# A chunked mLSTM stage rewritten to take its heads two at a time

## The reference

```
    log_d = jnp.where(lower, b[..., :, None] - b[..., None, :] + li[..., None, :], -jnp.inf)
    m_t = jnp.maximum(a, jnp.max(log_d, axis=-1))
    s = jnp.einsum('bhctk,bhcsk->bhcts', qc, kc) * jnp.exp(log_d - m_t[..., None])
    e_int = jnp.exp(a - m_t)
    num = (jnp.einsum('bhcts,bhcsv->bhctv', s, vc)
           + e_int[..., None] * jnp.einsum('bhcvk,bhctk->bhctv', C_prev, qc))
    den = jnp.sum(s, axis=-1) + e_int * jnp.einsum('bhck,bhctk->bhct', n_prev, qc)
    h = num / jnp.maximum(jnp.abs(den), jnp.exp(-m_t))[..., None]
...
        C_new = a[..., None, None] * C + e[..., None, None] * Cl
        n_new = a[..., None] * n + e[..., None] * nl
```

## Time and profile before

| what | value |
|---|---|
| median of three runs | 3321.8 us |
| time of the profiled execution | 3317.97 us |
| its span | 3316.2 us |
| TensorE busy in the span | 86% |
| VectorE busy | 52% |
| ScalarE busy | 35% |
| GpSimd busy | 25% |
| mean granted TensorE clock | 0.904 of full |

### The profile page before, as it was taken

The page is one execution under the profiler, slowest core; times in us unless marked ns, Lnnn a source line. Parts: engine busy times, 40 slices in busy tenths (PEclk is TensorE's granted clock), DMA queues, the critical chain, the costliest instruction groups (busy, mean ns, idle before and its releaser), DMA issues. The chain is left out here.

```text
span 3316.2 us, 39108 instructions
## 1 busy us (share of the span) xinstructions
PE 2861.8 (86%) x12086; PEld 2025.9 (61%) x12087; DVE 1726.0 (52%) x2710; ACT 1168.1 (35%) x1598; POOL 840.4 (25%) x1036
## 2 busy tenths in 40 slices
PE   4999969968787999999999993998987999883897
PEld 4455446647536777777777772446664666673776
DVE  3667845556535556756666554036644111435653
ACT  1100011123205556656666553005513111213653
POOL 0100021122173333333343332038320000103333
PEclk9999955569798999999999996999998999986999
DMA  5321100003316878978888865300011111316873
GB/s 217 103 102 54 54 0 1 1 29 142 152 65 226 276 225 271 316 252 300 306 274 295 249 165 168 113 0 1 27 15 51 38 44 33 135 70 223 306 232 59
DMA packets 159184, 463.49 MB, mean 140 GB/s; under 512 B 37964, under 2 KB 67264, under 8 KB 138328
## 3 DMA queue, kind: packets, MB, share of 16 engines
q1 hardware_dynamic: 115816, 358.12, 29.2%
q0 software_dynamic: 43264, 104.02, 13.1%
HBM read 414.31 MB, written 91.62 MB: 153 GB/s over the span
## 5 line engine op out<-in xcount | busy, mean ns | idle before, releaser
L1829 DVE TENSOR_TENSOR moe_low<-moe_raw,moe_high 128x2048 fp32r<-128x2048 f32 x160 | 359.5, 2288 | 80.6 <-ACT moe_high L1774 80.6
L1739 PE MATMUL psum<-moe_high,moe_xg_high 128*128 128x512 f32 x960 | 389.9, 406 | 6.1 <-issue 3.1
L1741 PE MATMUL psum<-moe_high,moe_xg_low 128*128 128x512 f32 x960 | 378.3, 394 | 0.0
L1740 PE MATMUL psum<-moe_low,moe_xg_high 128*128 128x512 f32 x960 | 375.5, 391 | 0.0
L1774 ACT ACTIVATE moe_high<-moe_raw 128x2048 fp32r<-128x2048 f32 x160 | 297.5, 1914 | 0.1
L1675 POOL DMA_INDIRECT moe_acc<-moe_y_blk,moe_is_now x97 | 216.2, 2229 | 303.6 <-DMA moe_acc<-moe_y_blk,moe_is_now 273.0
L1786 ACT ACTIVATE moe_y_blk<-psum,row_w 128x1024 f32 x124 | 138.1, 1113 | 232.7 <-DMA moe_acc<-moe_y_blk,moe_is_now 129.1
L1726 PE MATMUL psum<-moe_high_down,moe_hid_high 128*128 x488 | 208.3, 427 | 12.7 <-DVE moe_hid_low L1838 12.6
L1713 PE MATMUL psum<-ident,moe_xg 128*128 128x128 f32 x976 | 132.5, 280 | 96.8 <-DMA moe_xg<-moe_rows,moe_ig_now 96.8
L1739 PEld LDWEIGHTS psum<-moe_high,moe_xg_high 128*128 128x128 f32 x960 | 181.7, 189 | 43.1 <-issue 4.8
L1741 PEld LDWEIGHTS psum<-moe_high,moe_xg_low 128*128 128x128 f32 x960 | 180.8, 188 | 43.1
(11 more groups left out here) (574 smaller groups left out, 5305.3 us busy)
## 6 DMA issues: line engine op xcount, KB each, us to landing
moe_raw<-in_we_gate SPq DMA_DIRECT2D x64, 1024.0 KB, 7.7
moe_raw<-in_we_up SPq DMA_DIRECT2D x64, 1024.0 KB, 11.4
moe_raw<-in_we_down SPq DMA_DIRECT2D x64, 1024.0 KB, 7.5
moe_raw<-in_w_e_gate SPq DMA_DIRECT2D x16, 1024.0 KB, 7.0
moe_raw<-in_w_e_up SPq DMA_DIRECT2D x16, 1024.0 KB, 10.1
moe_raw<-in_w_e_down SPq DMA_DIRECT2D x16, 1024.0 KB, 8.7
w_ring<-in_w_in SPq DMA_DIRECT2D x12, 1024.0 KB, 7.3
wada<-in_w_ada SPq DMA_DIRECT2D x8, 1024.0 KB, 10.5
```

Source lines behind the costliest of these rows:

```text
L1739: pe.matmul(to, x_hi, R(of_k(w_hi, k)), start=(k == 0), stop=False)
L1740: pe.matmul(to, x_hi, R(of_k(w_lo, k)), start=False, stop=False)
L1741: last = pe.matmul(to, x_lo, R(of_k(w_hi, k)), start=False, stop=(k == KD - 1))
L1829: dve.tensor_tensor(R(low[:, at:at + 2048]), raw[r][:, part], hi, ALU.subtract).then_inc(w_low, 1)
```

## The change

The list of units becomes a list of pairs: chunk step j, direction d, pair of heads k, 40 in all; p is the index of a pair and v = p - 8 counts the 32 with outputs. The two heads of a pair, i = 0 and 1, have their keys and queries on partitions 0 to 63 and 64 to 127.

- The two local products go to the two column halves of bank 7, and one DVE instruction over 128 partitions updates the state of both heads. `EA2` holds their factors side by side. Bank 7 is the only one for local products, so that the local products of p wait for the state of p - 1.
- The two score products, and the two state products, go to the two row halves of the array and to two banks each.
- The running maxima of all four heads of a step and a direction are spread by one product of 512 columns (L801) every second pair, with `NM4`, in which each head's rows stand apart, and `of_group`. DVE adds the mask to the four at once (L887); E is now the bias of ACT's four exponentials (L853).
- DVE's product with the scores, the sum, and the three steps for the divisor are one instruction for two heads. ACT's scaling (L865), POOL's scaling and the final division (L920, L922) stay one instruction per head.

```
-    units = [(j, d, h) for j in range(STEPS) for d in range(2) for h in range(H1)]
+    pairs = [(j, d, k) for j in range(STEPS) for d in range(2) for k in range(H1 // 2)]
...
+                def maxima(g):
+
+                    pe.matmul(s.bank[6][:, :], of_group[:, NC * 2 + g:NC * 2 + g + 1].to_broadcast([NCOL, P]), NM4[:, :, :],
+                              start=True, stop=True).then_inc(maxima_done, 1)
+
                 def scores(v):
...
+                    for i in range(2):
+                        last = pe.matmul(s.bank[i][:, 0:P], s.qkT[lanes(i), 2 + k, t0:t0 + P], s.qkT[lanes(i), k, t0:t0 + P],
+                                         start=True, stop=True)
+                    last.then_inc(scores_done, 1)
...
+                    if p < PS:
+                        pe.wait_ge(wv_ready, 2 * (p + 1))
+                        if p >= 1:
+                            pe.wait_ge(state_moved, p)
+                        for i in range(2):
+                            h = 2 * k + i
+                            last = pe.matmul(s.bank[7][lanes(i), 0:W], s.k_tok[:, tile_of(j, d), h * DK:(h + 1) * DK],
+                                             wv[:, p % 2, i, :], start=True, stop=True)
+                        last.then_inc(local_done, 1)
                     if v >= 0:
...
                         if v >= 2:
                             pe.wait_ge(combined, v - 1)
+                        pe.wait_ge(state_moved, p - H1 + 1)
+                        for i in range(2):
+                            pe.matmul(s.bank[bank + i][:, 256:256 + W], s.qkT[lanes(i), k, t0:t0 + P], state[lanes(i), d, k, :],
+                                      start=True, stop=True)
                         pe.wait_ge(pt_ready, v + 1)
+                        if v + 1 < NV:
+                            scores(v + 1)
+                        for i in range(2):
+                            last = pe.matmul(s.bank[bank + i][:, 0:W], pt[:, v % 2, i, :], s.v_aug[:, tile_of(j, d), 2 * k + i, :],
+                                             start=True, stop=True)
+                        last.then_inc(num_done, 1)
+                        if v % 2 == 0 and v + 2 < NV:
+                            pe.wait_ge(masked, v // 2 + 1)
+                            maxima(v // 2 + 1)
...
+                for p, (j, d, k) in enumerate(pairs):
+                    v = p - P0
+                    if v % 2 == 1 and 0 <= v + 1 < NV:
+                        mask((v + 1) // 2)
                     if 0 <= v + 1 < NV:
                         weights(v + 1)
                     if v >= 0:
+                        dve.wait_ge(inter_ready, 2 * (v + 1))
+                        H, D2 = hsum[:, v % 2, :, :], dn[:, v % 2, :, :]
+                        dve.tensor_tensor(H, both(out_banks(v))[:, :, 0:W], inter[:, v % 2, :, :], ALU.add).then_inc(combined, 1)
...
+                    if p < PS:
+                        dve.wait_ge(local_done, p + 1)
+                        C = state[:, d, k, :]
+                        dve.scalar_tensor_tensor(C, C, EA2[:, j, d, k:k + 1], s.bank[7][:, 0:W],
                                                  ALU.mult, ALU.add).then_inc(state_moved, 1)
```

More of the change, by code:

```diff
@@ L844, in _, with exps @@
[L844 to L851, removed]
-                        act.activation(inter[:, v % 2, :], s.bank[2 + v % 2][:, 256:256 + W], ACT.Copy,
+                def exps(g):
+                    j, d, _ = pairs[P0 + 2 * g]
+                    act.wait_ge(masked, g + 1)
+                    for h in range(H1):
+                        one = decay[:, g % 2, h, :]
+                        act.activation(one, one, ACT.Exp, bias=s.E[:, j, d, h:h + 1]).then_inc(exp_ready, 1)
@@ new lines, in _ @@
+                exps(0)
+                for v in range(NV):
+                    j, d, k = pairs[P0 + v]
+                    if v % 2 == 1 and v + 1 < NV:
+                        exps(v // 2 + 1)
+                    act.wait_ge(num_done, v + 1)
+                    if v >= 2:
+                        act.wait_ge(combined, v - 1)
+                    for i in range(2):
+                        h = 2 * k + i
+                        act.activation(inter[:, v % 2, i, :], s.bank[out_banks(v) + i][:, 256:256 + W], ACT.Copy,
@@ L857, in _ @@
                 c = s.dve_c
-                c.link(dve, dve.memset(state[:, :, :, :], 0.0))
-                dve.wait_ge(masks_set, 2)
-                def decay(v):
-                    j, d, h = out_unit(v)
+                heads = lambda i: s.EA[lanes(i), :, :, :].rearrange("p j d (k i) -> p (j d k) i", i=2)[:, :, i]
+                unit = s.ident[0:NCOL, 0:NCOL]
+                c.then(dve.memset(state[:, :, :, :], 0.0))
+                for i in range(2):
+                    c.then(dve.tensor_copy(EA2[lanes(i), :, :, :].rearrange("p j d k -> p (j d k)"), heads(i)))
@@ new lines, in _ @@
+                c.then(dve.tensor_reduce(of_group[:, :], unit.rearrange("p (g h) -> p g h", h=H1), AX_X, ALU.add))
+                c.link(dve, dve.tensor_reduce(of_head[:, :], unit.rearrange("p (g h) -> p h g", h=H1), AX_X, ALU.add))
+                for h in range(H1):
+                    c.then(dve.tensor_scalar(NM4[:, h, :], s.NMT[:, :], of_head[:, h:h + 1], None, ALU.mult))
+                c.wait(dve)
+                dve.sem_inc(maxima_set, 1)
+                dve.wait_ge(masks_set, 2)
```

121 lines of the change are left out of this document (46 added, 75 removed).

## The result

Four runs of each kernel on the same chip: 3270.4 us after (3266.42 to 3272.6) against 3321.07 us before (3315.33 to 3322.37), a ratio of 0.9849 [0.9832, 0.9866]. The change saves 50.7 us of the median.

What follows compares the result with a forecast made beforehand. PE's queue, 7.06 us for two heads, was the bound, giving way to a ring of about 5.65 us. Stage -50 us and clock -10 gave 3318 - 60 = 3258, 3262 by the median; predicted 3260 us, range 3238 to 3285.

Steps and rivals of the forecast that it cites:

- What bounds the kernel before: In the stage, PE's queue is the limit: 3.53 us a unit, 7.06 us for two heads, at 1.2 GHz.
- Two heads at once: On PE, products of two heads in different array halves overlap wholly; local pair 0.62 us, state and scores 1.16.
- Rival 2: On PE, pairs of heads don't overlap: ring 6.95 us, stage -10 us, time 3308 us; chance 7%.
- The ring: One pair passes through PE, ACT and DVE before the next starts: 5.59 us, 5.71 in the second half, against 7.06.
- Rival 4: A ring somewhat longer, 6.1 us, with no help from the clock: 12 us more, about 3280 us; chance 12%.
- What lies beside it: Mask, exponentials, maxima, POOL's scalings and DVE's preparations are hidden beside the ring; the maxima with 0.5 us to spare.
- Start and end: First pair's products end near 468.9 us, 27 rings take 153, the stage's last write is near 636: -50 us.
- The clock, -10 us: In the stage, a quarter of 27 rings run at 2.4 GHz, each 1.4 us shorter: -10 us, bounds 0 and -20.
- Rival 3: No overlap on PE, each product costing 0.62 or 0.73 us: ring 8.2 us, stage +28, about 3346 us; chance 3%.
- turning point: The ring decides: over 7.06 us the change loses, as two units were in flight before and one pair is now.
- The rule on modes: On PE, mode changes drain the engine; with three changes replacing ten, the sum is the same by rule and by row.
- The rule on evacuation: PSUM evacuation becoming the bottleneck needs no rival of its own: ACT and DVE hold 2.5 of the ring's 5.65 us.

Runs made afterwards that it cites:

- e2: The changed kernel with PE's products of the two heads written so that products of one shape are not neighbours, one pair left by oversight; ratio 1.001 to the kernel before.
- e6: The changed kernel with the maxima of four heads from four products of 128 columns in place of one of 512; ratio 0.9849 to the kernel before.
- e4: The changed kernel with extra products that nobody reads, put into PE's pause to raise the clock; ratio 0.9794 to the kernel before.
- e5: The changed kernel itself, unaltered, run again on another chip; ratio 0.9857 to the kernel before.
- e1: The changed kernel with DVE's state update moved ahead of its combination of the pair; ratio 0.968 to the kernel before.
- e9: The changed kernel with DVE's state update ahead of the combination, and DVE's sum and divisor done per head; ratio 0.975 to the kernel before.

## Why the prediction was right, and where it was off

- **What bounds the kernel before.** PE's queue, 7.06 us for two heads. It rests on the rows of before: PE busy for 216.52 of 216.54 us, and no wait of PE's matmuls for another engine in that stretch. (The 3.7 us that the prediction names are waits of the weight loads, PEld.) That the products cost the same 0.62 and 0.73 us in e2 bears it out; that e2 comes back to the time of before (1.001) does not, since its limit is a ring.
- **Two heads at once.** Right: the first instructions of the two heads start 0.005 to 0.007 us apart in L824, L833 and L808, and the start of four instructions to the next product is 0.63, 0.59 and 0.57 us for the three pairs; 0.62 and 1.16 for the last two together had been worked out. Rival 2 (no overlap, 3308) fell.
- **The ring.** 5.59 and 5.71 us forecast, 5.65 and 5.79 measured in most rings of each half. The parts: the hand-over from DVE to PE 0.15 against 0.04 (the prediction took it from a hand-over of PE to ACT), the divisor 0.59 against 0.64, ACT 0.69 against 0.70, all others within 0.01. Rival 4 (6.1) fell. The prediction had L824 waiting some 2.5 us on most pairs: it does so on half of them (2.64), and behind a maxima product, which fills part of the pause, 0.93; 49.0 us in all. No term of the sum hung on it.
- **What lies beside it.** Mask, exponentials, maxima, POOL and DVE's preparation (444.22 to 446.4 us, POOL's first scaling at 452.92) delay nothing. For the maxima e6 shows it apart.
- **Start and end.** The first values products end at 469.72 us (468.9 forecast), the 27 rings hold 152.8 us (153 forecast; 154.1 without the clock's help in two of them), the rest takes 12.9 us (14.3 forecast), and the last write is at 635.41 against "near 636": -50.7 us against -50. That it comes so near owes something to luck: 0.8 us late at the start, 1.4 early at the end, and 1.3 that belong to the clock.
- **The clock, -10 us.** This is the term that was mis-sized. "A quarter of 27 rings" was to run at 2.4 GHz; the windows show 3.41 us, from 471.02 to 474.43. Two rings gained by it, 4.62 and 5.40 us against 5.65: 1.3 us. The price of a ring (1.4 us) was about right: 1.03 measured in a ring that had it in part, 1.3 in e4. The count was a guess, drawn from one rise in the attention; here one of some 14 long even runs was followed by a rise, and e5 has two rises among its rings. Two executions of this kernel have 3.4 and 13.7 us of it. Of the total's error of 10 us this term is 9.
- **Rival 3** (slower, ring of 8.2) fell, as two heads do run at once. Its price was tried in e2, which keeps them apart by their order: 7.52 us, and a time within about 0.2% of before. What the price lacked was the overlap of L817 and L807. Its turning point, 7.06 us, fits: a ring a little above it, 7.52 and 7.66, gave a stage a little longer, 224.7 us against 219.0.
- **The rule on modes.** "TensorEngine Tiling (Array Packing)", Tiling Modes, in the Trainium skill has a change of mode drain the array. The runs agree that a change costs (0.30 us at 1.2 GHz of each product alone, nothing between e6's four neighbours of one shape). That this is the draining the page speaks of is not shown; nor is how much of what the change gained on PE comes from fewer such changes.
- **The rule on evacuation** was waved aside as adding no rival. "TensorEngine Tiling (Array Packing)", PSUM Bottleneck, in the Trainium skill says that reading results out may become the bottleneck once tiling has made TensorE faster. No run here shows that as throughput: in the kernel after DVE is busy for 76 of 168 us, and what limits is its place in the ring. In e1 at the higher clock (DVE busy for 12.45 of 17.07 us) and in e9 the chain through DVE and ACT holds up the odd pairs, which comes nearer to it.

What the prediction saw and did not draw the consequence from: the ring passes through the combination only because of DVE's order. Moving one instruction (e1) took 57.5 us more off the stage, 50.6 of them at one clock; the whole change took off 50.9.

Open: what decides when the clock rises. It was up for 0 to 75 us of the stage in kernels whose work differs little, and for different times in two executions of one program. A second PSUM bank for the local product, which would let it run ahead, wasn't tried: all eight banks are in use.

## What to carry to other kernels

When one engine's queue is the bound and work is halved on it, look for the ring that appears next: follow one item from engine to engine in program order until it comes back, and sum durations and hand-overs; here that gave the new pace to a little over 1%. Then ask which instruction in the ring is there only because of where it is written; moving it can be worth as much as the packing. And compare queues pair by pair, not by their averages: in e9 an average of 3.80 us hid the 2.95 us of every second pair. Price an uncertain help such as the clock apart from the rest, and near zero if no stretch of the same stage shows it.

## What the runs showed of the hardware that was not expected

- Neighbouring products that have the same shape and lie in different row halves run at once whatever they are for: L817 and L807 in e2 start at 536.81 and 536.82, and each has two instructions.
- A float32 product of 128 columns whose neighbours have another shape costs 0.73 us at 1.2 GHz; four neighbours of 128 columns cost 1.91 in all, as one of 512 does. Nothing is lost between the values products and the maxima either, though one contracts over 128 rows and the other over 80: in e6's trace the last instruction of L842 and the first of L803 start 0.21 us apart.
- Granted clock: PE busy for 115.60 of 166.92 us had 3.4 us at 1.00; with fillers, 111.59 of 148.85 had 75 us.
- A DVE instruction on two columns (scalar_tensor_tensor) takes 0.16 us, the tensor_scalar on one column 0.21.
